# Streaming-encoder block on one core: split weight tiles kept in DRAM and loaded again by the later blocks

## What is computed

```
mod  = silu(c) @ ada_w + ada_b                      # six vectors of 1024: shifts, scales, gates
h    = modulate(rmsnorm(x), shift_a, scale_a)
proj = h @ w_in                                     # 1024 x 4104
mixed = concat(retention(4 heads), gated_delta(4 heads))   # chunks of 64 tokens, states carried on
x    = x + gate_a * (mixed @ w_out)                 # 1024 x 1024
h    = modulate(rmsnorm(x), shift_m, scale_m)
x    = x + gate_m * (square(relu(h @ w_ff1)) @ w_ff2)      # 1024 x 4096 and 4096 x 1024
out  = rmsnorm(x)
```

## Time and profile before

| what | value |
|---|---|
| median of three runs | 2794.85 us |
| the profiled execution, own time | 2797.37 us |
| its span, first to last instruction | 2795.5 us |
| TensorE busy, share of the span | 2709.8 us, 97% |
| GpSimd busy | 1667.8 us, 60% |
| VectorE busy | 1507.9 us, 54% |
| ScalarE busy | 1058.0 us, 38% |
| mean DMA rate over the span | 111 GB/s |
| mean granted TensorE clock | 0.991 |

### The profile page before, as it was taken

One profiled execution on the slowest core, in us unless ns is written; L12 is line 12 of the kernel. 1 busy time (PEld: TensorE's weight loads), 2 busy tenths in 40 slices (PEclk: granted clock), 3 DMA queues, 4 the chain that ended last, 5 costly groups with the idle time before them and its releaser, 6 DMA issues.

```text
span 2795.5 us, 36085 instructions
## 1 busy us (share of the span) xinstructions
PE 2709.8 (97%) x13344; PEld 2265.4 (81%) x13344; DVE 1507.9 (54%) x2423; ACT 1058.0 (38%) x1831; POOL 1667.8 (60%) x1260
## 2 busy tenths in 40 slices
PE   5999999999999999999999999999999999999998
PEld 4777787878888887888888888888888888888886
DVE  5878667464748556554546446573554563322223
ACT  3533332444333524353344433343333333443332
POOL 3745553666656756576655755675555566665653
PEclk9999999999999999999999999999999999999999
DMA  7333334332334223422233323422222223222232
GB/s 277 113 132 137 132 128 153 138 116 92 110 113 132 100 79 109 136 87 87 87 117 102 110 83 98 152 80 95 87 83 87 87 86 137 98 95 96 97 128 83
DMA packets 98094, 311.56 MB, mean 111 GB/s; under 512 B 11520, under 2 KB 11520, under 8 KB 95872
## 3 DMA queue, kind: packets, MB, share of 16 engines
q1 hardware_dynamic: 67248, 246.85, 26.1%
q10 hardware_dynamic: 30672, 62.40, 6.6%
HBM read 285.09 MB, written 24.12 MB: 111 GB/s over the span
## 4 chain that ended last, share of the span: by engine, by line
PE 84%; DVE 9%; issue 3%; POOL 2%; DMA 1%; ACT 1%; ACTq 0%; SPq 0%; DVEq 0%; POOLq 0%
PE acc L509 24%; PE acc L511 24%; PE acc L510 24%; PE pm L544 6%; PE pm L549 2%; DVE mixing L1232 1%; DVE x L1513 1%; POOL mT L1690 1%; POOL w L1681 1%; DVE mixing L1229 1%; PE pm L670 1%; PE pm L640 1%; DMA mixing<-in_ada_w 1%; PE pm L645 1%; PE pm L656 0%
## 5 line engine op out<-in xcount | busy, mean ns | idle before, releaser
L1681 POOL TENSOR_TENSOR w<-raw,w 128x512 fp32r<-128x512 f32 x832 | 1124.4, 1354 | 938.3 <-ACT w L752 935.4
L752 ACT ACTIVATE w<-raw 128x512 fp32r<-128x512 f32 x832 | 521.0, 627 | 768.4 <-PE acc L511 726.7
L509 PE MATMUL acc<-mT,w 128*128 128x512 f32 x1536 | 623.7, 406 | 10.5 <-POOL mT L1690 3.4
L511 PE MATMUL acc<-mT,w 128*128 128x512 f32 x1536 | 602.4, 392 | 0.0
L510 PE MATMUL acc<-mT,w 128*128 128x512 f32 x1536 | 601.3, 391 | 0.0
L509 PE MATMUL acc<-hid,w 128*128 128x512 f32 x864 | 348.8, 404 | 2.2 <-DVE ffs L1473 1.4
L509 PEld LDWEIGHTS acc<-mT,w 128*128 128x128 f32 x1536 | 291.0, 189 | 69.6 <-POOL mT L1690 5.2
L511 PEld LDWEIGHTS acc<-mT,w 128*128 128x128 f32 x1536 | 289.9, 189 | 62.7
L511 PE MATMUL acc<-hid,w 128*128 128x512 f32 x864 | 337.6, 391 | 0.0
L510 PE MATMUL acc<-hid,w 128*128 128x512 f32 x864 | 336.9, 390 | 0.0
L510 PEld LDWEIGHTS acc<-mT,w 128*128 128x128 f32 x1536 | 291.1, 190 | 54.1 <-issue 1.0
(11 more groups left out here) (231 smaller groups left out, 3702.0 us busy)
## 6 DMA issues: line engine op xcount, KB each, us to landing
raw<-in_w_all SPq DMA_DIRECT2D x416, 512.0 KB, 3.5
ada_late<-in_ada_w SPq DMA_DIRECT2D x32, 512.0 KB, 5.2
xr<-in_xT ACTq DMA_DIRECT2D x48, 256.0 KB, 3.4
mixing<-in_ada_w SPq DMA_DIRECT2D x8, 1024.0 KB, 9.6
proj_kept<-ffs ACTq DMA_DIRECT2D x32, 256.0 KB, 2.0
out<-io ACTq DMA_DIRECT2D x32, 256.0 KB, 2.4
mixed_kept<-mixing ACTq DMA_DIRECT2D x28, 256.0 KB, 2.0
xr<-mixed_kept ACTq DMA_DIRECT2D x28, 256.0 KB, 2.7
```

Source lines behind the costliest of these rows:

```text
L509: e.matmul(bank, whi, x[:, 0, :], start=first, stop=False)
L511: m = e.matmul(bank, wlo, x[:, 0, :], start=False, stop=last)
L752: e.activation(w2[:, 0, local % HALVES, :], raw[:, tile % NRAW, local % 2 * NT:(local % 2 + 1) * NT], ACT.Copy).then_inc(S["w_hi"], 1)
L1681: e.tensor_tensor(w2[:, 1, local % HALVES, :], raw[:, tile % NRAW, local % 2 * NT:(local % 2 + 1) * NT], w2[:, 0, local % HALVES, :].bitca ...
```

## The change

A tile is split only at its first use (104 of 416 tiles; `SPLIT_RANK` numbers them). SP then stores both parts of each half to a DRAM tensor `w_kept` (`store`). For each of the other 312 uses, SP loads the two halves from `w_kept` straight into the slots of `w2`; ACT and POOL do nothing for them, and PE waits for the landing. The four semaphores `slot0` to `slot3` count stores and loads of each slot. To make room for them, some semaphores that served the gates and the first inverse are merged; their waits keep their meaning.

```diff
+SPLIT_RANK, KEPT_BY = {}, {}
+for _g, _tile in enumerate(TILES):
+    _w = weight_index(_tile)
+    if _w not in KEPT_BY:
+        KEPT_BY[_w] = _g
+        SPLIT_RANK[_g] = len(SPLIT_RANK)
+SPLIT_TILES = sorted(SPLIT_RANK)
...
+        w_kept = nc.dram_tensor("w_kept", (len(SPLIT_TILES), 2, P, 2, NT), F32, kind="Internal").ap()
...
+        SLOTSEM = (S["slot0"], S["slot1"], S["slot2"], S["slot3"])
...
             def load(g):
-                if g >= NRAW:
-                    e.wait_ge(S["w_lo"], 2 * (g - NRAW) + 2)
-                e.dma_start(raw[:, g % NRAW, :], w_all[weight_index(TILES[g])]).then_inc(RAWSEM[g % NRAW], 16)
+                if g in SPLIT_RANK:
+                    r = SPLIT_RANK[g]
+                    if r >= NRAW:
+                        e.wait_ge(S["w_lo"], 2 * (r - NRAW) + 2)
+                    e.dma_start(raw[:, r % NRAW, :], w_all[weight_index(TILES[g])]).then_inc(RAWSEM[r % NRAW], 16)
+                else:
+                    maker = KEPT_BY[weight_index(TILES[g])]
+                    for half in range(2):
+                        local, made = 2 * g + half, 2 * maker + half
+                        e.wait_ge(SLOTSEM[made % HALVES], 16 * (made // HALVES + 1))
+                        e.wait_ge(S["w_used"], local - HALVES + 1)
+                        if (local - HALVES) // 2 in SPLIT_RANK:
+                            e.wait_ge(SLOTSEM[local % HALVES], 16 * (local // HALVES))
+                        e.dma_start(w2[:, :, local % HALVES, :].bitcast(F32), w_kept[SPLIT_RANK[maker], half]).then_inc(
+                            SLOTSEM[local % HALVES], 16)
+
+            def store(g):
+                for half in range(2):
+                    local = 2 * g + half
+                    e.wait_ge(S["w_lo"], 2 * SPLIT_RANK[g] + half + 1)
+                    e.dma_start(w_kept[SPLIT_RANK[g], half], w2[:, :, local % HALVES, :].bitcast(F32)).then_inc(SLOTSEM[local % HALVES], 16)
...
             for g in range(NRAW, len(TILES)):
+                if g - 2 in SPLIT_RANK:
+                    store(g - 2)
                 load(g)
...
-                if k % 4 == 0:
-                    e.wait_ge(S["w_lo"], local + 1)
+                if k % 4 == 0 and g in SPLIT_RANK:
+                    e.wait_ge(S["w_lo"], 2 * SPLIT_RANK[g] + half + 1)
+                elif k % 4 == 0:
+                    e.wait_ge(SLOTSEM[local % HALVES], 16 * (local // HALVES + 1))
...
             def hi(local):
-                tile = local // 2
-                e.wait_ge(RAWSEM[tile % NRAW], 16 * (tile // NRAW + 1))
+                if local // 2 not in SPLIT_RANK:
+                    return
+                r = SPLIT_RANK[local // 2]
+                if local % 2 == 0:
+                    e.wait_ge(RAWSEM[r % NRAW], 16 * (r // NRAW + 1))
                 if local >= HALVES:
                     e.wait_ge(S["w_used"], local - HALVES + 1)
-                e.activation(w2[:, 0, local % HALVES, :], raw[:, tile % NRAW, local % 2 * NT:(local % 2 + 1) * NT],
+                if (local - HALVES) // 2 in SPLIT_RANK:
+                    e.wait_ge(SLOTSEM[local % HALVES], 16 * (local // HALVES))
+                e.activation(w2[:, 0, local % HALVES, :], raw[:, r % NRAW, local % 2 * NT:(local % 2 + 1) * NT],
                              ACT.Copy).then_inc(S["w_hi"], 1)
...
             def lo(local):
-                tile = local // 2
-                e.wait_ge(S["w_hi"], local + 1)
+                if local // 2 not in SPLIT_RANK:
+                    return
+                r = SPLIT_RANK[local // 2]
+                e.wait_ge(S["w_hi"], 2 * r + local % 2 + 1)
```

More of the change, by code:

```diff
@@ L223 @@
 const_in lmask_in cs_in par_in mod_par_in host_consts
-raw0 raw1 w_hi w_lo w_used
+raw0 raw1 w_hi w_lo w_used slot0 slot1 slot2 slot3
 ada0 ada1 ada2 ada3 late0 late1 late2 late3 silu_c ada_parts piece_used mod_used mod_cols mod_ready
@@ L227 @@
 hf_ready h_hi h_lo h0_even h0_odd x0_ready
-own_steps u_turned nq_ready oct_masked oct_steps eye8_ready
-wg_split gate_rows gate_copied gate_out gate_steps gate_exp
+own_steps u_turned nq_ready oct_masked oct_steps
+wg_split gate_pe gate_copied gate_steps gate_exp
 proj_evac kept_evac kept_out0 kept_out1 kept_in out_evac ff1_relu ff1_evac hid_hi hid_lo ff2_evac
@@ L235 @@
 gt_out sqk_ready sqq_ready ss_steps nk_ready k_nat v_nat q_ready
-kk_out attn_ready lt_ready lvl_mask u_first t_ready x_out x_ready y_out t_next u_next
+kk_out attn_ready lt_ready lvl_mask ut_first x_out x_ready y_out t_next u_next
 negc_ready gvar silu_v mod_steps gates_done ks_out r_ready tr_out vnew_ready upd_out g_state o2_out
@@ L534, in gate_rows @@
                     m = e.matmul(bank[0:16, :], wgs[:, 1, k, :], x[:, 1, k, :], start=False, stop=k == KT - 1)
-                m.then_inc(S["gate_rows"], 1)
+                m.then_inc(S["gate_pe"], 1)
             def gate_columns(m, bank):
                 e.wait_ge(S["gate_copied"], m + 1)
-                turn(bank, gateT).then_inc(S["gate_out"], 1)
+                turn(bank, gateT).then_inc(S["gate_pe"], 1)
             def four(bank, lhs, rhs):
@@ L609, in mix @@
                         e.wait_ge(S["k_nat"], n + 1)
-                        e.wait_ge(S["t_ready"], n + 1)
+                        e.wait_ge(S["ut_first"], 2 * n + 2)
                     else:
@@ L618, in mix @@
                     else:
-                        e.wait_ge(S["u_first"], n + 1)
+                        e.wait_ge(S["ut_first"], 2 * n + 1)
                         e.wait_ge(S["attn_ready"], n + 1)
@@ L1168, in gates_copy @@
             def gates_copy(m, bank):
-                e.wait_ge(S["gate_rows"], m + 1)
+                e.wait_ge(S["gate_pe"], 2 * m + 1)
                 e.tensor_scalar(gateT[0:16, :], bank[0:16, :], one, None, ALU.mult).then_inc(S["gate_copied"], 1)
@@ L1176, in gates @@
                 if k == 0:
-                    e.wait_ge(S["gate_out"], m + 1)
+                    e.wait_ge(S["gate_pe"], 2 * m + 2)
                 else:
@@ L1331, in mix @@
                     if n == 0 and i == 0:
-                        e.wait_ge(S["eye8_ready"], 1)
+                        e.wait_ge(S["host_consts"], 4)
                     before = inv8 if i else eye8.unsqueeze(1).to_broadcast([P, SUB, OCT])
@@ L1342, in mix @@
                                     lmask[:, 1, :].rearrange("p (b j) -> p b j", j=OCT).unsqueeze(1).to_broadcast(
-                                        [P, SUB, P // OCT, OCT]), ALU.mult).then_inc(S["u_first"], 1)
-                    e.wait_ge(S["u_first"], n + 1)
-                    e.transpose(T, U).then_inc(S["t_ready"], 1)
+                                        [P, SUB, P // OCT, OCT]), ALU.mult).then_inc(S["ut_first"], 1)
+                    e.wait_ge(S["ut_first"], 2 * n + 1)
+                    e.transpose(T, U).then_inc(S["ut_first"], 1)
                 if s == 27:
@@ L1537, in _ @@
             e.wait_ge(S["const_in"], 32)
-            e.tensor_reduce(eye8, ident.rearrange("p (b j) -> p j b", j=OCT), AX.X, ALU.add).then_inc(S["eye8_ready"], 1)
+            e.tensor_reduce(eye8, ident.rearrange("p (b j) -> p j b", j=OCT), AX.X, ALU.add).then_inc(S["host_consts"], 1)
             e.wait_ge(S["host_consts"], 3)
@@ L1677, in lo @@
             def lo(local):
-                tile = local // 2
-                e.wait_ge(S["w_hi"], local + 1)
-                e.tensor_tensor(w2[:, 1, local % HALVES, :], raw[:, tile % NRAW, local % 2 * NT:(local % 2 + 1) * NT],
+                if local // 2 not in SPLIT_RANK:
+                    return
+                r = SPLIT_RANK[local // 2]
+                e.wait_ge(S["w_hi"], 2 * r + local % 2 + 1)
+                e.tensor_tensor(w2[:, 1, local % HALVES, :], raw[:, r % NRAW, local % 2 * NT:(local % 2 + 1) * NT],
                                 w2[:, 0, local % HALVES, :].bitcast(F32), ALU.subtract).then_inc(S["w_lo"], 1)
```

## The result

The changed kernel takes 2804.34 us in the median of 16 runs (2795.48 to 2811.25), the kernel before 2793.12 us. The ratio is 1.0046, with a 95% interval of 1.0035 to 1.0057: slower by about 11 to 13 us, just inside the 0.5% that was called "same". One of the 16 runs of the kernel before took 11492.29 us and is left out of the ratio, as is one of 7026.73 us in a later set. A second set of runs gave 1.0041 (1.0027 to 1.0055).

A forecast was written before the change was run, and what follows sets the result against it. PE, busy 2709.8 of 2795.5 us, was taken as the bound. 14 + 1 - 6 - 3.4 = +5.6 us on 2797.4 gave 2803, forecast as 2801 us because that execution is 2.5 us above the median; range 2780 to 2824.

The forecast's parts named there:

- same: Whole kernel: a time of 2781 to 2809 us, about 0.5% or 14 us from no change; chance 0.48.
- What bounds the kernel: Whole span: PE is busy 2709.8 of 2795.5 us, so a cheaper weight path can give back only PE's idle time.
- Order in SP's queue: Mostly up to 523 us: transfers behind the wait for reused second halves come late, costing PE 14 us in sum.
- worked example in window 1: Tiles 30 and 31: five transfers make `raw` land at 287.1, ACT stands, and PE loses 2.9 us (0 to 6).
- tile 28 then 29: Window 1, reused tile then new tile: no loss, as ACT's work there has 3 us and more of slack.
- The clock: TensorE's granted clock falls after PE pauses of 3 us: 1 us added.
- Window 3: All tiles reused; part 28 of `ada_w` lands at 429, DVE wants it at 427.30: 1 us lost (0 to 5).
- Window 4: With reused halves gone, gaps in POOL's run let DVE in and PE's pause shrinks: -6 us (0 to -9.7).
- Traffic from window 8 on: Windows 8 to 16: halves land in 3.5 to 5.2 us against 8.2 available, so PE waits nothing for them.
- POOL's low parts of `mT`: 1133 to 2355 us: PE's four waits at the starts of windows 8 and 12 go, -3.4 us (0 to 4.9).
- The third case: Whole kernel: POOL's halves no longer hold DVE up and ACT's standing is hidden; -18, 2777 us; chance 0.18.
- Before window 0: Tiles all new; two stores ahead make `raw` 3 us later each time: 1.5 us lost (0 to 5).

The follow-up runs named there:

- raw_first: Changed kernel with the raw load of the next new tile issued ahead of the reused tile's halves in SP's queue: 2785.82 us, ratio 0.9972 to the kernel before.
- all_ahead: raw_first with the stores of the tile before a reused one also issued ahead of its halves: 2777.76 us, ratio 0.9936 to the kernel before.
- ada_ahead: all_ahead with the parts of `ada_w` also issued ahead of the reused halves: 2768.94 us, ratio 0.9915 to the kernel before.
- second profile: The changed kernel run and profiled once more, unaltered: median 2807.88 us, ratio 1.0041 to the kernel before; the profiled execution took 2810.74 us.
- split_67_71: Changed kernel with five reused tiles of window 4 (67 to 71) split as before: 2809.94 us, ratio 1.0061 to the kernel before.
- stores_only: Kernel before plus the 208 stores alone, every tile split and nothing loaded again: 2794.38 us, ratio 1.0000.
- split_to_w7: Changed kernel with all 144 tiles up to window 7 split as before, reused loads only from window 8 on: 2793.25 us, ratio 0.9997 to the kernel before.
- split_to_w3: Changed kernel with all 56 tiles up to window 3 split as before, reused loads from window 4 on: 2782.04 us, ratio 0.9958 to the kernel before.

## Why the prediction was right, and where it was not

*Direction and size.* Forecast 2801 us and "same", measured 2804 us. That the time came out so close is in part luck: the net is small because two larger sums nearly cancel, and both were sized too small. Losses up to the point of window 3 were put at 1.5 + 2 + 4 + 4 = 11.5 us and 1 us for the clock, and are 24.0 us in the profile. From there to the end the forecast was 1 + 1.5 - 6 - 3.4 = -6.9 us, and it is -21.3 (-13.9 in the second profile).

*What bounds the kernel.* Right. PE is busy for 96 to 98% of the span in all runs. Its idle time up to 523 us is 35.2 + 38.8 = 74 us; I had about 68, and under 54 the order of the queue would have been harmless.

*Order in SP's queue.* The mechanism is right and is shown by raw_first, all_ahead and ada_ahead: one move after the other takes the waits of ACT for `raw`, of ACT for stores and of DVE for `ada_w` away, with the same traffic. The places and sizes are not right. Window 0 was put at 2 us and takes 10.9; windows 1 and 2 at 4 us each and take 5.8 and 3.8, all with the clock's share in them. The price of the queue was too low: for the six transfers issued when tile 17 is done (the second half of tile 19, two parts, two stores, `raw` of tile 20) my prices give 2.0 + 6 x 1.5 = 11 us from the tile's end, and the trace has 13.1 (from 192.8 to 205.9). It was not the issuing: `raw` was issued at 196.42 and ACT could start only at 205.93. What holds the transfers back is not told apart by any run.

The worked example in window 1 did not come true in its place. ACT stands 4.20 us for `raw` of tile 31, at 299.46, and PE waits for nothing there. PE's waits for this queue in window 1 were two others: the copy of `X` behind tile 27, with 5.71 us where I had 1.2, and the place "tile 28 then 29", which I had put at nothing because ACT had 3 us of slack. ACT stands 9.58 us there, DVE stands behind ACT, and PE behind DVE:

```profile
286.33 0.63 ACT L790 ACTIVATE w<-raw 128x512 fp32r<-128x512 f32 x1 [9.58 <-DMA raw<-in_w_all]
288.30 1.80 DVE L1312 TENSOR_TENSOR mixing<-mixing,cs 128x512 f32<-128x512 f32 x1 [2.22 <-ACT mixing L959]
292.09 0.80 PE L678 MATMUL pm<-rvv,mixing 128*128 128x128 f32 x2 [3.21 <-DVE rvv L1439]
```

*The clock.* 1 us was forecast for it. From point 0 to point 3 it went from 0.98 to 0.95 and 0.94 in the two profiles. By these rows the lower clock takes 0.02 x 284 = 6 us before, and 0.05 x 304 = 15 and 0.06 x 307 = 18 us after: some 9 and 12 us more, less what of it fell into idle time. PE's idle time there grew by 15 us, where the forecast had 10. So the clock is the term that was missed most. It goes with the spread of the runs: 2795.48 us at a clock of 0.992, 2811.25 at 0.988.

*Window 3.* Forecast +1 us, but from its point to that of window 4 the changed kernel gained 4.0 us in one profile and lost 3.1 in the other. PE's idle time is 1.2 and 2.2 us more than before, so the forecast's sign was right for it; what turned it over was the clock, 0.99 in one and 0.93 in the other against 0.94. Of the kernels in the table only ada_ahead has less idle time here than before, 0.0 against 3.5 us: POOL splits nothing in this window, and no part of `ada_w` is late.

*Window 4.* The pause went whole: forecast -6 with the bound -9.7, measured -9.5. That the reused halves before the run decide is shown by split_67_71. My reason for it was wrong: I expected gaps in POOL's run that let DVE in. POOL's timeline of the changed kernel has none from the moment when DVE's operation arrives (L1730 makes low parts of `mT`, L1721 is the split, L1757 and L1760 another product):

```profile
622.52 2.74 POOL L1730 TENSOR_TENSOR mT<-io,mT 128x512 fp32r<-128x512 f32 x2
625.23 1.74 POOL L1721 TENSOR_TENSOR w<-raw,w 128x512 fp32r<-128x512 f32 x1
626.93 1.73 POOL L1757 TENSOR_TENSOR rot<-pr,cs 128x512 f32<-128x512 f32 x1
628.63 3.17 POOL L1721 TENSOR_TENSOR w<-raw,w 128x512 fp32r<-128x512 f32 x2
631.75 1.73 POOL L1760 TENSOR_TENSOR rot<-pr,cs 128x512 f32<-128x512 f32 x1
```

Its operations take 1.6 to 1.7 us each and not 1.25, and DVE's operations come in between. In the kernel before, DVE's operation arrives at the same place of POOL's order, at 604.97, in the first of these two parts of `mT`:

```profile
604.70 2.55 POOL L1690 TENSOR_TENSOR mT<-io,mT 128x512 fp32r<-128x512 f32 x2
```

What differs is the moment within that POOL operation: 0.27 us after its start in the kernel before, 0.97 us in the changed one. All the traces fall into these two groups: the four with the long DVE operation (before, stores_only, split_to_w7, split_67_71) have 0.27 to 0.29 us, the seven without it 0.96 to 0.98 us. The ten splits shift the two engines against each other by that much. Why this moment decides stays open.

*Traffic from window 8 on.* Right: a half lands after 3.7 us and PE waits for landed halves 1.2 us in the whole run.

*POOL's low parts of `mT`.* Forecast -3.4, and split_to_w7 has -3.3 from window 8 on, but the agreement is luck. The four waits of the earlier trace rows are gone (they stood in the middle of windows 8 and 12, near 1205 and 1873, and not at their starts). In their place PE waits for DVE at other points of the same windows, first in the changed kernel, then in split_to_w7 (1133 to 2355; us, times, longest):

```profile
PE acc L542 <- DVE x L1499: 2.6, 4, 1.4
PE acc L553 <- DVE x L1510: 4.8, 4, 2.5
```

In this stretch split_to_w7 has the same idle time as the kernel before, 4.9 us. Where its gain comes from, and why the changed kernel has -5.5 from window 8 on and raw_first -6.2, is not explained by any run.

*DVE and POOL.* The third case's mechanism is real: DVE's busy time is 1507.9 us before, 1507.1 in stores_only, 1387.8 in split_to_w7, 1364.9 in split_to_w3 and 1334.7 in the changed kernel, with the same 2423 instructions; it falls with the number of halves that POOL splits. The Trainium skill, page "SBUF — State Buffer", section "Who interferes with whom", says that a DVE instruction with two SBUF inputs contends with a GpSimd instruction that reads SBUF; the trace agrees by these 173 us. The case asked for ACT's standing to be hidden, and it was not. In ada_ahead ACT waits for `raw` 36.9 us in all and not 192.5, and PE's idle time from 120 to 523 falls from 20.6 to 12.6 us, where the case had 7 us less; the ratio is 0.9915, and the median of 2768.94 us lies under the 2777 us of that case. How much of that is DVE's time and how much the earlier parts of `ada_w` is not told apart.

*Before window 0.* Forecast 1.5 us, measured 1.0 to 4.1 at the point of window 0; split_to_w3, split_to_w7 and stores_only, which only add stores up to there, stand at +2.5 to +2.7 at the next one.

## What to carry to other kernels

When a prefetch changes from "when a buffer is free" to "when its last user has finished", it becomes a late wait in the program of the queue that issues it; everything written behind it in that program inherits the wait, whether it needs it or not. List what stands behind it before counting bytes: here three moves in SP's order, with the same DMAs, turned 0.4% slower into 0.85% faster. The same may hold on ACT, which works in order too: there a split for later use stood ahead of a copy that PE was waiting for. No run here moved it.

## What the runs showed of the hardware

A DVE operation of 128x512 that takes 0.48 us alone waited 8.2 us beside a run of POOL operations that followed each other without a gap, in the kernel before, stores_only, split_67_71 and split_to_w7 alike (8.69 to 8.72 us). In the changed kernel POOL's run at that place has no gap either, but DVE's operation starts 0.97 us into a POOL operation, not 0.27, and takes 0.62 us. So it was not held up by one POOL operation but by seven. An unbroken run is not enough for that: at 1199.19 in the kernel before, the same DVE operation met one and took 0.80 us. Why one arrival loses to all of them and another only to the one that is running, no run tells.

The issue of a DMA took SP 0.52 us for a half (median of 624) and 0.51 us for a store, both with 2 KB rows in SBUF, and never less, against 0.33 us for a `raw` tile of the same 512 KB in the kernel before. In the changed kernel a `raw` tile took 0.61 us in the median (0.34 at least), so what else is in the queues counts as well, and the part of the row length is not shown by itself.
